# A hybrid attention and convolution layer on one core: sample index scores in two halves around the first tile's heads, convolution taps at other places, eight page numbers per load

## The reference, cut to what matters

```python
logits = jnp.einsum('bthd,bsd->bths', qi, ki)                  # 8 indexer heads of 64
score = jnp.einsum('bths,bth->bts', jax.nn.relu(logits), wi)   # weighted sum over heads
_, sel = lax.top_k(score, topk)                                # 256 keys per query
...
glu = cu[..., :CONV_CH] * jax.nn.sigmoid(cu[..., CONV_CH:])
c, conv_state = causal_dwconv(glu, conv_prev, w_dw, b_dw)      # 512 channels, 31 taps
```

## Time and profile before

| what | us |
|---|---|
| median of 3 runs (their range) | 4341.82 (4334.56 to 4343.23) |
| profiled execution | 4338.67 |
| its span | 4337.1 |
| busy in the span: PE, DVE, ACT, POOL | 3967.7, 2649.8, 1086.5, 799.9 |

### The profile page before, as it was taken

One profiled execution on the slowest core, in us unless ns is written; L12 is line 12 of the kernel. 1 busy time (PEld: TensorE's weight loads), 2 busy tenths in 40 slices (PEclk: granted clock), 3 DMA queues, 4 the chain that ended last, 5 costly groups with the idle time before them and its releaser, 6 DMA issues. The chain is left out here.

```text
span 4337.1 us, 41426 instructions
## 1 busy us (share of the span) xinstructions
PE 3967.7 (91%) x13224; PEld 2030.6 (47%) x13224; DVE 2649.8 (61%) x4865; ACT 1086.5 (25%) x2166; POOL 799.9 (18%) x1086
## 2 busy tenths in 40 slices
PE   8948898999999999999989999999977989999997
PEld 3532343444344444443434444434333447777775
DVE  1777677888763458897784359999687321321213
ACT  1113202212135023122155122221224542220211
POOL 4332003444410000000000029994000000000000
PEclk9959999999999999999999999999988999999998
DMA  4315113444431111121111111112110094122121
GB/s 160 111 53 126 64 58 110 134 133 132 149 108 37 70 59 68 58 84 64 67 55 44 68 59 68 60 65 75 63 55 1 1 252 127 59 69 73 65 76 45
DMA packets 157587, 349.75 MB, mean 81 GB/s; under 512 B 21440, under 2 KB 103872, under 8 KB 135776
## 3 DMA queue, kind: packets, MB, share of 16 engines
q1 hardware_dynamic: 124112, 274.74, 19.1%
q0 software_dynamic: 33296, 72.68, 5.6%
HBM read 334.33 MB, written 55.16 MB: 90 GB/s over the span
## 5 line engine op out<-in xcount | busy, mean ns | idle before, releaser
L1022 PE MATMUL ps<-arena,weight_ring 128*128 128x512 f32 x3936 | 1723.4, 598 | 35.5 <-DVE arena L2401 16.6
L1022 PEld LDWEIGHTS ps<-arena,weight_ring 128*128 128x128 f32 x3936 | 751.1, 192 | 997.4 <-issue 968.4
L2127 DVE TENSOR_SCALAR_CACHE_REDUCE t_t<-arena,threshold_tried 128x384 bf16<-128x384 f32 (+13 forms) x448 | 661.8, 1477 | 10.6
L1020 PE MATMUL ps<-arena,weight_ring 128*128 128x288 f32 x2592 | 639.2, 409 | 16.4 <-DVE arena L1951 11.1
L1020 PEld LDWEIGHTS ps<-arena,weight_ring 128*128 128x128 f32 x2592 | 496.8, 192 | 156.2 <-issue 12.7
L1035 PE MATMUL ps<-arena,weight_ring 128*128 128x512 f32 (+1 forms) x1360 | 520.4, 545 | 3.8 <-DVE arena L2029 3.1
L2385 DVE SCALAR_TENSOR_TENSOR arena<-arena,ffn_conv_w 128x512 f32<-128x512 f32 x352 | 281.8, 801 | 339.9 <-ACT ffn_carry L1873 245.8
L1035 PEld LDWEIGHTS ps<-arena,weight_ring 128*128 128x128 f32 x1360 | 251.9, 205 | 264.7 <-issue 259.5
L958 POOL DMA_DIRECT2D out_y<-arena x4 | 3.5, 885 | 1924.6 <-DVE arena L1951 1853.5
L1857 ACT COPY arena<-ffn_carry 128x2 f32<-128x2 f32 x176 | 33.9, 192 | 1174.9 <-PE ps L1022 816.5
L2356 DVE TENSOR_TENSOR arena<-arena,ps 128x512 f32<-128x512 f32 (+1 forms) x96 | 67.3, 701 | 329.9 <-PE ps L1020 198.1
(11 more groups left out here) (227 smaller groups left out, 3692.8 us busy)
## 6 DMA issues: line engine op xcount, KB each, us to landing
weight_ring<-in_w_pairs SPq DMA_DIRECT2D x165, 1024.0 KB, 4.8
weight_ring<-in_w_down SPq DMA_DIRECT2D x64, 704.0 KB, 4.1
gathered_k<-in_k_t POOLq DMA_DIRECT2D x256, 64.0 KB, 2.1
gathered_v<-in_v_t POOLq DMA_DIRECT2D x256, 64.0 KB, 2.1
arena<-gathered_k SPq DMA_DIRECT2D x64, 256.0 KB, 5.4
arena<-gathered_v SPq DMA_DIRECT2D x64, 256.0 KB, 3.4
arena<-in_x_t SPq DMA_DIRECT2D x8, 1024.0 KB, 9.0
gathered_idx<-in_idx_t POOLq DMA_DIRECT2D x256, 32.0 KB, 1.9
```

The source lines that it names most:

```text
L1020: ins = mm(bank[:, half, :], w, src[:, half, :], start=start, stop=stop)
L1022: ins = mm(bank, w, src, start=start, stop=stop)
L2127: step(W.tensor_scalar(junk, S, TRY[:, :].bitcast(F32), 0.0, ALU.is_ge, ALU.add, accum_out=COUNT[:, :]))
```

## The change

1. The sample index is split: units 0 to 15 run on PE before the heads of tile 0, units 16 to 32 behind them. Each half sums its own two sequence pairs in PP[0..3]; ACT copies the first half's sums to SBUF, and DVE adds the second half's from PSUM (`sample_logits`). PE's heads now wait for the first copies, its convolution mean for DVE's additions.
2. The empty place "pre" of tile 0 gets room for 36000 ns of tries on DVE, beside the first half.
3. All 124 tap instructions of tile 0 move into its projection: 16, 18, 18 and 16 behind the four gated units, then 8 and four times 12 between the ropes. The first two channel groups are done tap after tap, the last two in turn.
4. The sample's taps stand between the heads of tile 0 (3, 3, 3, 4, 4, 4, 4 and 3 taps of four groups; three more behind them).
5. Four of the sample's tries move to a new place "scale", between the scaling of tile 0 and that of the sample; the gated units of tile 1 get 9 instead of 13, of which the last stands in the place of the selection, ahead of it.
6. POOL loads eight page numbers at a time, and loops half as often (also for the later gather of keys and values).

```diff
-EARLY_TAPS = (2, 5, 8, 11, 14)
+EARLY_TAPS = [(0, k) for k in range(CONV_W)] + [(1, k) for k in range(CONV_W)]
+EARLY_TAPS += [(j, k) for k in range(CONV_W) for j in (2, 3)]
+EARLY_ROOM = (16, 34, 52, 68, 76, 88, 100, 112, 124)
+SAMPLE_FILLS = ((0, 3), (3, 6), (6, 9), (9, 13), (13, 17), (17, 21), (21, 25), (25, 28))
...
     if kind == "pre":
-        return 0, 0
+        return (36000, 99) if g == 0 else (0, 0)
...
-    spare = [("out", 0, k, 0) for k in range(3)] + [("out", 0, k, 0) for k in range(3, KT_D) for _ in range(2)]
+    spare = [("scale", 0, 0, 0) for _ in range(4)] + [("out", 0, k, 0) for k in range(3)] + [("out", 0, k, 0) for k in range(3, KT_D) for _ in range(2)]
     spare += [("rope", 1, p, 0) for p in (0, 0, 1, 2, 3, 4)]
-    spare += [("glu", 1, j, m) for j in range(4) for m in range(2) for _ in range(2)]
+    spare += [("glu", 1, 0, 0)] + [("glu", 1, j, m) for j in range(4) for m in range(2)]
...
-                with pl.Fori(first // 4, last // 4) as i:
-                    page = [pl.value_load(PTAB[0:1, bass.ds(i * 4 + x, 1)], min_val=0,
-                                          max_val=a["idx_t"].shape[0] - 1) for x in range(4)]
-                    for x in range(4):
+                with pl.Fori(first // 8, last // 8) as i:
+                    _, page = nc.values_load_multi_w_load_instructions(
+                        PTAB[0:1, bass.ds(i * 8, 8)], engines=[pl.engine], min_val=0,
+                        max_val=a["idx_t"].shape[0] - 1)
+                    for x in range(8):
...
# PE: attention of tile 0, then the index
-                    pe.wait_ge(rope_done, 10 * (sample.q + 1))
-                    pe.wait_ge(tok_used, sample.tok0 + 1)
+                    pe.wait_ge(s_read, 16)
+                    pe.wait_ge(sc_read, 4)
...
-            def sample_index():
+            def sample_index(first, last):
...
-                    ins = mm(PP[cc][64 * half:64 * half + 64, :], WS[:, bp, :], RL[u % 4][:, :], start=bp == 0,
-                             stop=bp == 3)
+                    ins = mm(PP[cc][64 * half:64 * half + 64, :], WS[:, bp, :], RL[u % 4][:, :], start=bp % 2 == 0,
+                             stop=bp % 2 == 1)
...
+                if first == 0:
...
+                    pe.wait_ge(wst_full, 1)
...
+                    pe.wait_ge(qs_full, 1)
+                else:
+                    pe.wait_ge(o_used, 8)
+                    pe.wait_ge(t_copied, tiles[0].mine[3].turns)
+                logits(first)
+                logits(first + 1)
                 pe.wait_ge(ws_full, 1)
-                for u in range(32):
-                    logits(u + 2) if u + 2 < 32 else None
+                for u in range(first, last):
+                    if u + 2 < last:
+                        logits(u + 2)
                     weigh(u)
+                if last < 32:
+                    return
...
             in_proj(sample, None)
+            sample_index(0, 16)
             for t in tiles:
...
                 if t.g == 0:
-                    sample_index()
-                    pe.wait_ge(sc_read, 5)
+                    sample_index(16, 32)
+                    pe.wait_ge(sc_read, 9)
                     conv_mean(t)
...
# ACT (the first half has the loop over units 0 to 15 and these copies)
-                for cc in range(4):
-                    ac.wait_ge(rl_used, 26 + 2 * cc)
-                    A.copy(SCs[:, cc * TILE:(cc + 1) * TILE], PP[cc][:, :]).then_inc(sc_read, 1)
+                if last == 16:
+                    for cc in range(4):
+                        ac.wait_ge(rl_used, 10 + 2 * cc)
+                        A.copy(SCs[:, cc * TILE:(cc + 1) * TILE], PP[cc][:, :]).then_inc(sc_read, 1)
...
# DVE
+                        else:
+                            early_taps(t, j)
...
+                    ve.wait_ge(conv_step, tapped[t.g, j])
+                    W.scalar_tensor_tensor(out=xc, in0=w, scalar=DWW[:, j, k:k + 1], in1=xc, op0=ALU.mult,
+                                           op1=ALU.add).then_inc(conv_step, 1)
+                tapped[t.g, j] = n.next(conv_step)
...
+            def early_taps(t, slot):
+                for j, k in EARLY_TAPS[EARLY_ROOM[slot - 1] if slot else 0:EARLY_ROOM[slot]]:
+                    conv_tap(t, j, k)
...
                     selection(("value", blk.b, jj, 0))
+                    if t.g == 0:
+                        conv_taps(sample, *SAMPLE_FILLS[i])
...
+            def sample_logits():
+                ve.wait_ge(sc_read, 4)
+                for cc in range(4):
+                    ve.wait_ge(rl_used, 26 + 2 * cc)
+                    S = SCs[:, cc * TILE:(cc + 1) * TILE]
+                    W.tensor_tensor(S, S, PP[cc][:, :], ALU.add).then_inc(sc_read, 1)
...
             spread_weights()
+            selection(("pre", 0, 0, 0))
...
                 if t.g == 0:
-                    conv_taps(t, EARLY_TAPS[-1], CONV_W)
-                    conv_taps(sample, 0, CONV_W)
+                    conv_taps(sample, SAMPLE_FILLS[-1][1], CONV_W)
+                    sample_logits()
                     conv_centre(t)
                     conv_centre(sample)
                     conv_scale(t)
+                    selection(("scale", 0, 0, 0))
                     conv_scale(sample)
```

More of the change, by code:

```diff
@@ L1776, in sample_queries, with sample_index @@
                 ins.then_inc(qs_full, 1)
-            def sample_index():
-                ac.wait_ge(wtr_full, 1)
-                A.copy(WS, PS[:, 7, 0:4 * NS].rearrange("p (s n) -> p s n", s=4)).then_inc(ws_full, 1)
-                for u in range(33):
+            def sample_index(first, last):
+                if first == 0:
+                    ac.wait_ge(wtr_full, 1)
+                    A.copy(WS, PS[:, 7, 0:4 * NS].rearrange("p (s n) -> p s n", s=4)).then_inc(ws_full, 1)
+                for u in range(first, last):
                     w = TILE if u < 32 else 4 * NS
@@ L1914, in _ @@
                 if t.g == 0:
-                    sample_index()
+                    sample_index(16, 33)
                     conv_variance(t)
@@ L1937, in _ @@
             n = Counts(ve)
-            aux, ropes = [0], [0]
+            aux, ropes, tapped = [0], [0], {}
             W = nc.vector
@@ L2076, in in_proj, with conv_tap @@
                     glu_pairs()
+            def conv_tap(t, j, k):
+                xc = t.xc(4 + j)[:, 0:t.n]
+                if t.sample:
+                    xc, w = t.seqs(xc), t.glu(j)[:, :, k:k + DEC_T]
+                else:
+                    w = t.glu(j)[:, 0, k:k + TILE]
+                if k == 0:
+                    ve.wait_ge(glu_done, 4 * t.q + j + 1)
+                    W.tensor_scalar(xc, w, DWW[:, j, 0:1], DWB[:, 0, j:j + 1], ALU.mult, ALU.add)\
+                        .then_inc(conv_step, 1)
+                else:
+                    ve.wait_ge(conv_step, tapped[t.g, j])
+                    W.scalar_tensor_tensor(out=xc, in0=w, scalar=DWW[:, j, k:k + 1], in1=xc, op0=ALU.mult,
+                                           op1=ALU.add).then_inc(conv_step, 1)
+                tapped[t.g, j] = n.next(conv_step)
@@ L2078, in conv_taps, with convolved @@
+            def convolved(t):
+                ve.wait_ge(conv_step, n.now(conv_step))
+                ve.sem_inc(convs_out if t.sample else conv_out, 4)
+            def early_taps(t, slot):
+                for j, k in EARLY_TAPS[EARLY_ROOM[slot - 1] if slot else 0:EARLY_ROOM[slot]]:
+                    conv_tap(t, j, k)
+                if EARLY_ROOM[slot] == len(EARLY_TAPS):
+                    convolved(t)
             def conv_taps(t, first, last):
-                mine = range(t.pe_conv, 4)
@@ L2081, in conv_taps @@
-                if not mine:
-                    return
                 for k in range(first, last):
-                    for j in mine:
-                        xc = t.xc(4 + j)[:, 0:t.n]
-                        if t.sample:
-                            xc, w = t.seqs(xc), t.glu(j)[:, :, k:k + DEC_T]
-                        else:
-                            w = t.glu(j)[:, 0, k:k + TILE]
-                        if k == 0:
-                            if j == t.pe_conv:
-                                ve.wait_ge(glu_done, 4 * (t.q + 1))
-                            W.tensor_scalar(xc, w, DWW[:, j, 0:1], DWB[:, 0, j:j + 1], ALU.mult, ALU.add)\
-                                .then_inc(conv_step, 1)
-                        else:
-                            ve.wait_ge(conv_step, n.now(conv_step, 1 - len(mine)))
-                            W.scalar_tensor_tensor(out=xc, in0=w, scalar=DWW[:, j, k:k + 1], in1=xc, op0=ALU.mult,
-                                                   op1=ALU.add).then_inc(conv_step, 1)
-                        n.next(conv_step)
+                    for j in range(4):
+                        conv_tap(t, j, k)
@@ L2101, in conv_taps @@
                 if last == CONV_W:
-                    ve.wait_ge(conv_step, n.now(conv_step))
```

(2 more changed lines are left out.)

23 lines of the change are left out of this document (13 added, 10 removed).

## The result

The changed kernel takes 4302.08 us (median of 4 runs, 4300.09 to 4303.91) beside 4342.52 for the kernel before on the same chip: a ratio of 0.9915, interval 0.9902 to 0.9927, or 40.4 us less. Its profiled execution took 4300.09 us, with a span of 4298.6; the spans differ by 38.5.

A forecast was written before the change was run, and what follows sets the result against it. PE and DVE were taken to bound the kernel in turns: attention at DVE's pace, the sample index at PE's. Terms -32.3, +1.0 and +3.5 sum to -27.8 us, giving a median of 4314.0, taken as 4313, range 4301 to 4331.

The forecast's parts named there:

- Taps: Tile 0's projection: the moved taps overrun two places, DVE is done about 105, PE stays unbroken; cost 0, at most 2.2.
- the pair's 0.79: Old trace: in a pair of such instructions on the same width, the second starts 0.79 us after the first.
- First half: Sample index before the heads: 16 units in 32.2 us plus 3.5 for low clock, ending near 290, beside DVE's tries.
- Heads: Tile 0's attention: DVE's tries done about 315, then seven halves without tries; 79 us after 291 instead of 107.
- Second half: Sample index behind the heads: 16 units in 32.2 us, 2.3 more to the mean, at 404.8 instead of 437.12.
- Page numbers: POOL's gather: eight numbers per load give a gap of 3.2 us, a group of 8.6, the end at 298.
- Scale: Four sample tries and preparation take 14.3 us in 12.83 idle; the sample's scaling comes 1.5 later; +1.0 us in all.
- Last try: Tile 1's gated units: the 32nd try stands ahead of the selection and adds its whole length, +3.5 us.
- The sum: Whole kernel: -32.3 for the earlier mean, +1.0 and +3.5 behind it, together -27.8 us.
- No half starved: Rival: POOL's stores or a late gather starve an index half; about 13 of 32 us return, 4326; chance 0.2.
- The heads weren't slow: Rival: fills or low clock delay every half of tile 0's heads, 94 us instead of 79; 4328; chance 0.1.
- PE reached the full level: Rival: PE stays at 1.2 GHz through both index halves, each unit costs 2.01 us more; 4374; chance 0.04.

The follow-up runs named there:

- the second comparison: The changed kernel run again as it is, beside the kernel before on the same chip: 4302.02 us, ratio 0.9916.
- the taps alone: The kernel before with only tile 0's tap instructions moved under the gated units and between the ropes: 4337.0 us, ratio 1.0000.
- the run with four pages: The changed kernel with the old load of four page numbers instead of eight: 4323.89 us, ratio 0.9969.
- an earlier selection: The changed kernel with the sample's selection behind the third head's second unit and tile 1's nine tries packed ahead of it: 4288.11 us, ratio 0.9884.
- spread tries: The kernel with the selection moved earlier, plus the sample tries ahead of the output projection spread into DVE's idle time: 4277.72 us, ratio 0.9858.
- sixteen pages: The changed kernel with sixteen page numbers per load instead of eight: 4300.16 us, ratio 0.9917.

## Why the prediction was right, point by point

The forecast of 4313 within 4301 to 4331 had the sign and the mechanisms; its sum was 27.8 us where 40.4 were measured (35.0 in the second comparison, 4337.05 to 4302.02), and the time stands at the fast end of the range, 1 us inside it. That it lies inside was in part luck: the range's lower end was drawn for heads at full clock (6 us less) and for scatter, and the heads were that much faster mainly for another reason, the smaller halves of block 1.

*Taps.* Right. 18 dependent taps took 14.13 us, 0.785 each, by the pair's 0.79; independent ones 45.13/68 = 0.66. They end at 104.25 for a forecast of about 105, PE is unbroken, and the taps alone give 1.0000. The Trainium skill ("VectorE: DVE Perf Modes", section "The DRAIN you can't avoid") says that a semaphore between chained Vector instructions costs nothing extra; by that they would have taken 0.66 too. Here a tap that waits for the one right before costs 0.12 more. Both kinds carry a semaphore wait in the code (`conv_tap`); they differ in that the tap that the independent ones wait for is four back.

*First half.* It ended at 287.8 instead of 290: the restart costs 5.38 - 2.79 = 2.6 us instead of 3.5, and products of one kind are quicker back to back than in turn: at the two ends of a half three units take 2.79 + 1.93 us, not 3 x 2.01. It bought nothing by itself, as DVE's tries still ended at about 315, the date forecast.

*Heads.* The mechanism was right, a term mis-sized: "six turnarounds of 7.9 and the last of 5, 52 us", plus "2 us" for the sample's taps. From 315.35 on the halves took 7.1, 5.4, 6.3, 8.0, 7.35, 8.35 and 5.8, 48.2 us in all. The rows of before, from 326.42 to 350.03, belong to blocks 2 and 3, and these repeated to a tenth (8.0, 7.35, 8.35); block 1, with fewer keys, had no half without tries in the old trace, and took 5.4 and 6.3. The last half took 5.8 instead of 5 as PE now waits 0.60 for DVE before the second half. Of the 2 us for the sample's taps in block 0, PE's timeline shows 0.61, its wait for the inverse that DVE computes behind them:

```profile
317.08 1.12 PE L1235 MATMUL ps<-const_mats,row_inv 128*64 128x128 f32 x8 [0.61 <-DVE row_inv L2311]
```

With 48.2 us for 54 the heads are 5.8 of the 8.4 us by which the mean is ahead of the forecast. Of the rest 1.7 are the second half, and about 1 lies in the sum itself, whose dates were rounded up on the way: 315 + 52 + 2 + 34.5 gives 403.5, not 404.8.

*Second half.* 32.8 us from its start to the mean instead of 34.5: the 16 units take 30.8 (to 394.3) instead of 32.2, by the same two ends.

*Page numbers.* The gap was 2.97 for a forecast of 3.2, the group 8.15 for 8.6, the end 288 for 298. The working was not quite right: the load is not "paid once". It is one instruction, but takes 0.572 us for eight numbers where one took 0.288, and the rest of the gap is cheaper than thought. From eight to sixteen the gap grows by 2.31 us, 0.29 a number. The date still was in the heads, and the run with four pages shows what it was worth.

*Scale.* From the mean to the first group of tile 1's projection 82.98 us instead of 80.92: +2.1 for a forecast of +1.0. The mechanism was right but smaller: the wait for the squares grew by 0.96 where 1.5 was worked out, and 0.6 came back in front of the output projection. What the forecast lacked is the clock: eight products of the convolution's projection (L1026) took 5.40 us at 402.68 (granted clock 0.72 from 402 to 405), while PE's timeline of the kernel before has, with the same idle time ahead and a granted clock of 1.00 from 443 to 446:

```profile
443.39 3.70 PE L1022 MATMUL ps<-arena,weight_ring 128*128 128x512 f32 x8 [1.74 <-DVE arena L2111]
...
518.04 10.14 PE L1043 MATMUL ps<-arena,weight_ring 128*128 128x512 f32 x16 [5.60 <-issue]
```

*Last try.* +3.47 in the wait for +3.5, and it goes with the try.

*The sum.* Up to the product behind the sample's selection: -40.7 + 2.1 + 3.3 = -35.3 (684.34 to 649.02). The other 3.2 of the spans' 38.5 is scatter: from that product to the end it is 3652.8 us before, 3649.6 in this profile and 3652.2 in the changed kernel's second one, whose gain of 35.0 is also what the steps add up to.

*The rivals.* No half starved; the price given to it (13 us) was too low, as the four pages cost 21.8. It was read from one starved wait, where the old trace has two, and at its late end it left out that the fourth sequence pair itself comes too late. The heads weren't slow, though PE still waits in their first two halves. PE reached the full level 6 us into the first half and kept it in the second.

## What to carry to other kernels

Moving work from an engine's busy stage to its idle one is worth nothing alone if another engine set that stage's end: here the split, the tries beside it, the taps out of its way and the page loads had to come together, and tries, taps and loads, each taken back by itself, cost 18 to 31 us. The split, the sample's taps between the heads and the four tries at "scale" weren't taken back by themselves, so what each is worth alone isn't shown. Price a stage without a disturbance by rows of the same size, block by block, not by the largest blocks alone. And date every transfer of every queue that the moved stage will meet; then look where the last of a spread-out series stands, for a step right in front of what is awaited costs its full length: an earlier selection and spread tries were worth another 24 us.

## What the runs showed of the hardware that was not expected

- One load of several register values on POOL's queue takes 0.288 us for one, 0.572 for eight and 1.058 for sixteen; the gap between groups of DMA issues is 3.03, 2.97 and 5.28 us for four single loads, one of eight and one of sixteen. Longer loads save little: 0.76, 0.37 and 0.33 us of gap for each number.
- The clock can fall behind a wait of 1.7 us in front of the convolution's projection (5.40 us for eight products) or not (3.70 before the change, with four and with sixteen pages). What tells the two apart stays open.
- Loads that share the DMA engines with another engine's stores land late: SP's key loads took 2.5 to 3.1 us before POOL's stores and 7.1 to 17.9 beside them (sixteen pages). Where PE needed such keys, it lost the wait and then units at the lower level behind it: with four pages 18.1 us of waits, some 4 of them the late gather, made the kernel 21.8 us longer.
